# Time mixer of a hybrid decoder block: the triangular inverse in two 32 x 32 blocks a head, with VectorE transposes, and a new order of the units

## The chip, the core and the metric

The kernel runs on one core of a Trainium2 chip. The metric is device time in microseconds of one execution. Engines: TensorE (PE), VectorE (DVE), ScalarE (ACT), GpSimd (POOL) and SyncE (SP), which issues the weight loads. Each works through its own queue in order; semaphores tie them together.

## The reference, cut to what matters

The program is one decoder block on 272 tokens (16 meta tokens and 256) of width 2048: layer norm, a projection, an RWKV-7 time mixer with 32 heads of 64, a causal pooling branch, a gated merge, and an expert channel mixer. The change touches the time mixer alone:

```python
def step(S, inp):
    r_t, w_t, k_t, v_t, kk_t, a_t = inp
    sa = jnp.einsum('bhij,bhj->bhi', S, -kk_t)
    S = (S * w_t[:, :, None, :]
         + sa[..., None] * (kk_t * a_t)[:, :, None, :]
         + v_t[..., None] * k_t[:, :, None, :])
    y_t = jnp.einsum('bhij,bhj->bhi', S, r_t)
    return S, y_t
...
y = rwkv7_scan(r_h, w_h, k_h, v_h, kk, a_h)
ym = jnp.mean(y, axis=-1, keepdims=True)
yv = jnp.mean(jnp.square(y - ym), axis=-1, keepdims=True)
y = ((y - ym) * lax.rsqrt(yv + GN_EPS)).reshape(B, T, RWKV_DIM) * gn_g + gn_b
```

`y_t` is linear in the values `v`, so values with their mean over a head's 64 channels taken out give a `y` with mean zero.

## The kernel before, in words

`rwkv_stage` takes the heads in 16 pairs: two heads fill the 128 partitions, and `by_head` issues one 64 x 64 product for each of them. The 272 tokens are padded to five chunks of 64. Inside a chunk the recurrence is solved in closed form, which needs the inverse of a unit triangular 64 x 64 matrix per chunk and head; from chunk to chunk the state S is carried (units r, u, s).

The inverse is built by doubling. Unit gr makes three grams: B by A (masked into `LT_st`), A by B (the start of the first factor `X_st`) and K by A (masked into `MT_st`). `Y_st`, the second factor, is X's transpose. At level i = 1 to 5 unit Z multiplies `LT_st` by `X_st`, DVE masks the result into `Z_st`, and unit W forms two products, Y by Z, added to `X_st` (not at level 5), and Z by Y, added to `Y_st`. All are 64 columns wide. Levels 4 and 5 leave out the first chunk.

Unit t turns B, K and V (`BKV_by_token`) by a product with the identity; V's product gives tokens by channels. After the chain, unit yc copies y out of PSUM, gm takes its mean by a product with ones (line 704), DVE subtracts it (line 925), ACT squares it (line 794), gv sums the squares (line 708), ge and gy normalise and gate.

Beside this runs the projection: unit f issues one of 16 steps of a tile as three products (line 188, `product`), 48 steps a turn; its weights come in halves that SP loads, ACT rounds (line 152) and DVE takes the remainder of (line 173), unit sp. Units e take a finished tile out of PSUM. Units lw, la, lg, nm, bo are full-width products of the low-rank paths, the norm of k and the bonus; kn, ex, ab are the ACT and DVE work for them.

The order is one table, `ORDER`, written by hand. `schedule` runs over it on each of PE, ACT and DVE, and each engine carries out the units that it knows. `STAGE` says how many turns a pair lags in a unit: f works on pair b while the low-rank units work on b - 1, the inverse on b - 2 and the chain on b - 3:

```python
for b in range(-1, PAIRS + 3):
    for name, i in ORDER:
        p = b - STAGE[name]
        if name in units and 0 <= p < (PAIRS + 4 if name in STREAM else PAIRS):
            units[name](i, p, p % 2)
```

Of the kernel before, what the change touches and what calls it, by code (L numbers as in the profile page):

```python
# [45 lines left out]
C_IOTA = C_LEV + 64 * (LEVELS - 1 + 1)  # L46
NCONST = C_IOTA + 16


# [142 lines left out]
def front_stage(k, w):  # L192

    nc = k.nc
    with ExitStack() as ctx:  # L195
# [265 lines left out]
def rwkv_stage(k, w):  # L461

    nc = k.nc
    with ExitStack() as ctx:
# [1333 lines left out]
```

## Time and profile before

| | |
|---|---|
| median of 3 runs | 2664.82 us (2664.28 to 2665.7) |
| profiled execution | 2663.81 us, span 2661.3 us |
| granted TensorE clock, mean | 0.986 |
| PE busy | 2255.4 us, 85% |
| DVE busy | 1566.4 us, 59% |
| ACT busy | 661.0 us, 25% |
| first and last gram of the time mixer | 102.11 us, 795.44 us |

A profile's rows name a line of the kernel, an engine, an operation and the tiles it writes and reads. PE rows with x20 are 20 instructions: an fp32 product counts as two, and `by_head` issues one for each head. Idle time in brackets is the engine's idle time just before, with what released it. Busy time of PE runs from a product's start to its modelled end, which is later than the start of the next one.

### The profile page before, as it was taken

How to read it: one execution, taken by the hardware profiler on the slowest of the kernel's cores; microseconds unless marked ns; L12 is line 12 of the kernel's file. 1: busy time of each engine (PE TensorE's matmuls, PEld its weight loads, DVE VectorE, ACT ScalarE, POOL GpSimd, SP SyncE). 2: the span in 40 equal slices, each digit the busy share in tenths (PEclk: the TensorE clock that was granted, in tenths of full speed). 3: DMA queues.
4: the chain of work that ended last, by engine and by line, in shares of the span. 5: the costliest groups of instructions: out<-in, count | busy, mean ns of one | idle time of the engine just before them, and what ended most of it. 6: DMA issues, size and time to landing. Idle time of an engine off the chain costs nothing.

```text
span 2661.3 us, 42121 instructions
## 1 busy us (share of the span) xinstructions
PE 2255.4 (85%) x17653; PEld 1593.7 (60%) x17653; DVE 1566.4 (59%) x2588; ACT 661.0 (25%) x1282; POOL 672.1 (25%) x541
## 2 busy tenths in 40 slices
PE   6989888988988999999898879897778778777776
PEld 6888888888887899997764434443223233222222
DVE  7576666667665545545685567666744544444445
ACT  4433333433332344443221111111100100000000
POOL 1000000000000000000154545455554555444442
PEclk9999999999999999999999999999999999999999
DMA  5422223222232676666599999999999999999997
GB/s 183 122 76 69 78 69 88 69 80 69 64 81 73 184 191 186 184 167 239 176 409 409 413 413 418 417 418 420 421 420 420 420 414 415 420 420 420 420 420 307
DMA packets 346507, 710.49 MB, mean 267 GB/s; under 512 B 13832, under 2 KB 270400, under 8 KB 279744
## 3 DMA queue, kind: packets, MB, share of 16 engines
q0 software_dynamic: 74176, 537.01, 48.9%
q1 hardware_dynamic: 271904, 170.59, 22.3%
q8 instruction: 140, 2.29, 0.4%
q14 instruction: 47, 0.39, 0.0%
q10 hardware_dynamic: 240, 0.21, 0.0%
HBM read 705.66 MB, written 2.10 MB: 266 GB/s over the span
## 4 chain that ended last, share of the span: by engine, by line
DMA 32%; PE 13%; DVE 2%; issue 2%; POOL 1%; DVEq 0%; ACT 0%; POOLq 0%; ACTq 0%
DMA down_rows<-in_v_table,experts 30%; PE bank L1534 10%; DMA up_rows<-in_u_table,experts 3%; PE bank L1483 2%; POOL down_rows L1471 1%; POOL up_rows L1465 1%; DVE up_rows L1635 0%; PE bank L1505 0%; ACT diagonal L1587 0%; PE bank L1499 0%; PE bank L1493 0%; DVE one_hot L1171 0%; DVE expert_sides L1177 0%; DVE side_index L1150 0%; DVE side_index L1143 0%
## 5 line engine op out<-in xcount | busy, mean ns | idle before, releaser
L1534 PE MATMUL bank<-down_rows,diagonal 128*128 128x512 f32 x2032 | 947.1, 610 | 246.5 <-DMA down_rows<-in_v_table,experts 210.0
L1635 DVE CUSTOM_DVE_ANT_0 up_rows<-up_rows,h 128x2048 f32<-128x2048 f32 x256 | 585.5, 2291 | 560.6 <-DMA up_rows<-in_u_table,experts 560.6
L1534 PEld LDWEIGHTS bank<-down_rows,diagonal 128*128 128x128 f32 x2032 | 374.1, 192 | 777.9 <-DMA down_rows<-in_v_table,experts 397.0
L1465 POOL DMA_INDIRECT up_rows<-in_u_table,experts x256 | 279.2, 1091 | 1347.4 <-POOLq L1189 1253.0
L1471 POOL DMA_INDIRECT down_rows<-in_v_table,experts x256 | 384.4, 1502 | 570.8 <-PE bank L1534 562.5
L173 DVE TENSOR_TENSOR w_half_rest<-w_half,w_half_high 128x1024 fp32r<-128x1024 f32 x224 | 273.6, 1223 | 260.1 <-ACT w_half_high L152 258.8
L188 PE MATMUL project<-hT_high,w_half_high 128*128 128x272 f32 x896 | 285.7, 319 | 1.4 <-PEq L195 1.4
L152 ACT CAST w_half_high<-w_half 128x1024 fp32r<-128x1024 f32 x224 | 234.4, 1049 | 192.6 <-PE merge_ps L188 163.9
L188 PE MATMUL project<-hT_high,w_half_rest 128*128 128x272 f32 x896 | 259.2, 289 | 0.0
L188 PE MATMUL project<-hT,w_half_high 128*128 128x272 f32 x896 | 258.5, 289 | 0.0
L1605 ACT ACTIVATE dots<-dots 128x4 f32<-128x4 f32 x64 | 13.1, 205 | 743.1 <-DVE dots L1635 743.0
L188 PEld LDWEIGHTS project<-hT_high,w_half_high 128*128 128x128 f32 x896 | 169.3, 189 | 8.8 <-issue 1.6
L188 PEld LDWEIGHTS project<-hT,w_half_high 128*128 128x128 f32 x896 | 169.5, 189 | 4.2
L188 PEld LDWEIGHTS project<-hT_high,w_half_rest 128*128 128x128 f32 x896 | 169.1, 189 | 0.0
L1587 ACT ACTIVATE diagonal<-constants,weights 128x128 f32<-128x128 f32 x256 | 81.9, 393 | 282.3 <-DVE weights L1642 282.3
L188 PE MATMUL merge_ps<-hT_high,w_half_high 128*128 128x256 f32 x512 | 144.5, 282 | 6.1 <-PEq L91 6.1
L188 PE MATMUL merge_ps<-hT,w_half_high 128*128 128x256 f32 x512 | 145.2, 284 | 0.0
L188 PE MATMUL merge_ps<-hT_high,w_half_rest 128*128 128x256 f32 x512 | 145.1, 283 | 0.0
L188 PEld LDWEIGHTS merge_ps<-hT_high,w_half_high 128*128 128x128 f32 x512 | 98.0, 191 | 6.5 <-issue 6.5
L188 PEld LDWEIGHTS merge_ps<-hT_high,w_half_rest 128*128 128x128 f32 x512 | 98.1, 192 | 0.0
L188 PEld LDWEIGHTS merge_ps<-hT,w_half_high 128*128 128x128 f32 x512 | 97.3, 190 | 0.0
L518 PE MATMUL invert<-X_st,LT_st 64*64 64x64 f32 x1472 | 58.6, 221 | 24.4 <-DVE X_st L902 24.2
(314 smaller groups left out, 3157.9 us busy)
## 6 DMA issues: line engine op xcount, KB each, us to landing
w_half<-in_w_in SPq DMA_DIRECT2D x176, 512.0 KB, 4.2
w_half<-in_w_branch_a SPq DMA_DIRECT2D x32, 512.0 KB, 4.1
out_w<-in_w_out SPq DMA_DIRECT2D x16, 1024.0 KB, 5.3
query_w<-in_w_q_peer SPq DMA_DIRECT2D x10, 1024.0 KB, 34.1
w_half<-in_w_branch_b SPq DMA_DIRECT2D x16, 512.0 KB, 4.1
out_w<-in_w_q_peer SPq DMA_DIRECT2D x6, 1024.0 KB, 36.2
up_rows<-in_u_table,experts POOLq DMA_INDIRECT x256, 16.5
down_rows<-in_v_table,experts POOLq DMA_INDIRECT x256, 15.9
```

Of the source, the lines that this page charges most:

```text
L152: self.nc.scalar.copy(self.w_high[g % 3][:].bitcast(F32R), self.w_raw[g % 3][:]).then_inc(self.s_rounded, 1)
L173: return eng.tensor_tensor(low.bitcast(F32R), x, high, ALU.subtract)
L188: mm = nc.tensor.matmul(out, a.bitcast(F32R), b.bitcast(F32R), start=start and n == 0, stop=stop and n == 2)
L518: mm = nc.tensor.matmul(out[h], wts[h], x[h], start=start, stop=stop)
L1465: pool.indirect_dma_start(ur[n % RU][:], None, w["u_table"][0], bass.IndirectOffsetOnAxis(ap=k.idx[:, t, h, j:j + 1], axis=0)).then_inc(s_ ...
L1471: pool.indirect_dma_start(vr[n % RV][:], None, w["v_table"][0], bass.IndirectOffsetOnAxis(ap=k.idx[:, t, h, j:j + 1], axis=0)).then_inc(s_ ...
L1483: mm = nc.tensor.matmul(pq[i][:, 0:SEQ], k.query_part(h, i, kt), k.h1T[:, kt, :], start=(kt == 0), stop=(kt == KT - 1))
L1534: mm = nc.tensor.matmul(acc[t][c][:], dg[n % RD][:], vr[n % RV][:, quarter(c)], start=False, stop=(n == last(t, c)), skip_group_check=True)
L1587: nc.scalar.activation(dg[n % RD][:], ident, ACT.Copy, scale=weights[:, n:n + 1]).then_inc(s_diag, 1)
L1605: nc.scalar.activation(x, x, ACT.Gelu).then_inc(s_gelu, 1)
L1635: v.tensor_tensor_reduce(ur[n % RU][:], ur[n % RU][:], k.h[:, n // (HEADS * TOPK), :], 1.0, 0.0, ALU.mult, ALU.add, dots[:, n:n + 1]).then ...
```

## The change

- The inverse is kept as the two 32 x 32 diagonal blocks of each head, side by side in 32 columns: `X_blocks` and `Y_blocks` are 5 x 32 wide. The A by B gram goes. Level 0 is now a Z product too (against a 32-column identity), and its result, masked, is X; Y is its transpose by `n.transpose`, which turns 32 x 32 blocks on DVE.
- Levels 1 to 4: Z (32 columns), a mask that spreads the result over the two blocks (`Z_st`, 64 columns), one product T (32 columns) added to Y, and X as the transpose of Y. The product Y by Z goes.
- Level 5 uses the off-diagonal block `LT_off`, which ACT cuts from the gram. ACT spreads Y's blocks into the 64-column `Y_st` (unit yf), and T of level 5 is added to its right half.
- The two products on R share one PSUM bank and one mask (`RBKT_st`).
- V is turned by a centring matrix instead of the identity. The mean product, the subtraction and unit gm go; ACT squares y straight from PSUM, before it copies it.
- The units stand in a new order. Unit nm's DVE part is a unit nr of its own.

```diff
+    c[:, C_LEV:C_LEV + CH] = s // HALF == t // HALF
...
+    c[:, C_CEN:C_CEN + CH] = (s == t) - 1.0 / HEAD
...
 ORDER = (
-    ("sp", 1), ("cv", 0), ("gr", 0), ("r", 0), ("t", 0), ("sp", 2), ("f", 6),
-    ("u", 0), ("rb", 0), ("s", 0), ("rk", 0), ("t", 1), ("kn", 0), ("f", 6),
-    ("r", 1), ("Z", 1), ("u", 1), ("lw", 0), ("sp", 3), ("f", 6), ("e", 0),
-    ("s", 1), ("W", 1), ("r", 2), ("Z", 2), ("u", 2), ("la", 0), ("sp", 4), ("f", 6),
-    ("s", 2), ("W", 2), ("r", 3), ("Z", 3), ("u", 3), ("lg", 0), ("sp", 5), ("f", 6),
-    ("ex", 0), ("s", 3), ("W", 3), ("r", 4), ("Z", 4), ("u", 4), ("nm", 0), ("f", 6), ("e", 1),
-    ("s", 4), ("W", 4), ("Z", 5), ("bo", 0), ("yc", 0), ("ahead", 0), ("f", 4),
-    ("ab", 0), ("W", 5), ("gm", 0), ("f", 4), ("gv", 0), ("f", 4), ("ge", 0), ("e", 2), ("gy", 0),
+    ("r", 0), ("gr", 0), ("sp", 1), ("t", 0), ("rb", 0), ("u", 0), ("t", 1), ("Z", 0), ("s", 0), ("sp", 2), ("f", 2),
+    ("lw", 0), ("f", 4),
+    ("Z", 1), ("cv", 0), ("r", 1), ("f", 2),
+    ("la", 0), ("u", 1), ("T", 1), ("f", 7),
+    ("lo", 0), ("kn", 0), ("sp", 3), ("lg", 0), ("s", 1), ("Z", 2), ("r", 2), ("T", 2), ("u", 2), ("f", 3),
+    ("sp", 4), ("nm", 0), ("f", 2),
+    ("s", 2), ("Z", 3), ("r", 3), ("nr", 0), ("T", 3), ("u", 3), ("f", 7),
+    ("s", 3), ("Z", 4), ("ex", 0), ("sp", 5), ("r", 4), ("T", 4), ("u", 4), ("bo", 0), ("f", 1),
+    ("e", 0), ("s", 4), ("Z", 5), ("yc", 0), ("ab", 0), ("f", 2),
+    ("yf", 0), ("gv", 0), ("ge", 0), ("T", 5), ("f", 18),
+    ("e", 1), ("ahead", 0), ("gy", 0), ("e", 2),
 )
...
@@ block.tensor
-                for n, lhs, rh in ((0, bst, ast[par]), (1, ast[par], bst), (2, kst, ast[par])):
+                for n, lhs in ((0, bst), (2, kst)):
                     for c in range(NCH):
-                        mm = by_head(inv[n][:, c * CH:(c + 1) * CH], lhs[:, c, :], rh[:, c, :])
+                        mm = by_head(inv[n][:, c * CH:(c + 1) * CH], lhs[:, c, :], ast[par][:, c, :])
...
-                    mm = by_head(low[:, m * CH:(m + 1) * CH], (bst, kst, vst)[n][:, c, :], turn)
+                    mm = by_head(low[:, m * CH:(m + 1) * CH], (bst, kst, vst)[n][:, c, :], center if n == 2 else turn)
...
                 for c in chunks(i):
-                    mm = by_head(inv[0][:, c * CH:(c + 1) * CH], lt[:, c, :], xs[:, c, :])
+                    mm = by_head(inv[2][:, c * HALF:(c + 1) * HALF], (lto if i == LEVELS - 1 else ltd)[:, c, :], xs[:, c, :] if i else eye)
...
-            def W_(i, p, par):
+            def T_(i, p, par):
                 wait(pe, q["Zst"], p * 5 + i)
                 wait(pe, q["Y"], p * LEVELS + i)
...
-                if i < LEVELS - 1:
-                    for c in chunks(i):
-                        mm = by_head(inv[2][:, c * CH:(c + 1) * CH], ys[par][:, c, :], zs[:, c, :])
-                    mm.then_inc(q["W"], 1)
-                for c in chunks(i):
-                    mm = by_head(inv[1][:, c * CH:(c + 1) * CH], zs[:, c, :], ys[par][:, c, :])
+                for c in chunks(i):
+                    mm = by_head(inv[1][:, c * HALF:(c + 1) * HALF], zs[:, c, :], yb[:, c, :])
...
-            def gm(_, p, par):
-                wait(pe, q["Yc"], p + 1)
-                nc.tensor.matmul(mean_ps, ones, yc[:], start=True, stop=True).then_inc(q["mean"], 1)
...
@@ block.scalar
                 wait(act, q["Yo"], p * 4 + 4)
+                nc.scalar.activation(ysq[:], y_ps, ACT.Square).then_inc(q["sqr"], 1)
                 nc.scalar.copy(yc[:], y_ps).then_inc(q["Yc"], 1)
...
+            def lo(_, p, par):
+                wait(act, q["Z"], p * LEVELS)
+                wait(act, q["maskT"], p + 1)
+                nc.scalar.activation(lto[:], c3(inv[0][:, 0:TP]), ACT.Copy, scale=upper).then_inc(q["off"], 1)
+
+            def yf(_, p, par):
+                wait(act, q["Y"], p * LEVELS + LEVELS - 1)
+                nc.scalar.activation(ys[par][:, :, 0:HALF], yb[:], ACT.Copy, scale=upper)
+                nc.scalar.activation(ys[par][:, :, HALF:CH], yb[:], ACT.Copy, scale=lower).then_inc(q["Yfull"], 1)
...
@@ block.vector
             def Z(i, p, par):
+                if i == 0:
+                    n.tensor_tensor(xs[:], c3(inv[2][:, 0:NCH * HALF], HALF), block_mask(C_M1, NCH), ALU.mult)
+                    d()
+                    n.tensor_tensor(xs[:], xs[:], block_mask(C_M1 + HALF, NCH), ALU.add).then_inc(q["X"], 1)
+                    d()
+                    n.transpose(flat(yb), flat(xs)).then_inc(q["Y"], 1)
+                    return
...
+                n.tensor_tensor(yb[:, c0:], yb[:, c0:], add, ALU.add).then_inc(q["Y"], 1)
+                d()
+                n.transpose(flat(xs, c0), flat(yb, c0)).then_inc(q["X"], 1)
```

Three places of the new order, for a turn in the middle. First PE, from unit s of chunk 1 to unit u of chunk 2, level 2 of the inverse; `chain` is the state's PSUM, `invert` the inverse's. Before:

```order
L518 MATMUL chain<-BKV_by_token 64x64 x2
L518 MATMUL chain<-U,BKV_by_token 64x64 x2
L518 MATMUL invert<-Z_st,Y_st 64x64 x10
L518 MATMUL invert<-Y_st,Z_st 64x64 x10
L518 MATMUL chain<-BKV_by_token,MT_st 64x64 x2
L518 MATMUL chain<-S,A_st 64x64 x2
L518 MATMUL chain<-R_st,S 64x64 x2
L518 MATMUL chain<-RKT_st,BKV_by_token 64x64 x2
L518 MATMUL chain<-RBT_st,U 64x64 x2
L518 MATMUL invert<-X_st,LT_st 64x64 x10
L518 MATMUL chain<-rhs,Y_st 64x64 x2
```

Now:

```order
L535 MATMUL chain<-BKV_by_token 64x64 x2
L535 MATMUL chain<-U,BKV_by_token 64x64 x2
L535 MATMUL invert<-X_blocks,LT_diag 64x32 x10
L535 MATMUL chain<-BKV_by_token,MT_st 64x64 x2
L535 MATMUL chain<-S,A_st 64x64 x2
L535 MATMUL chain<-R_st,S 64x64 x2
L535 MATMUL chain<-RBKT_st,BKV_by_token 64x64 x2
L535 MATMUL chain<-RBKT_st,U 64x64 x2
L535 MATMUL invert<-Y_blocks,Z_st 64x32 x10
L535 MATMUL chain<-rhs,Y_st 64x64 x2
```

T, with 32 columns, stands behind the 20 instructions of unit r, and X's transpose is needed only in the next Z; before, W stood in front of r, and its Z in front of the projection.

Second DVE, the start of the inverse of a pair. Before:

```order
L872 COPY chunk_decay<-decay_prod 128x5
L874 TENSOR_TENSOR LT_st<-invert,constants 128x320
L876 TENSOR_TENSOR X_st<-invert,constants 128x320
L878 TENSOR_TENSOR Y_st<-LT_st,constants 128x320
L879 TENSOR_TENSOR X_st<-X_st,constants 128x320
L881 TENSOR_TENSOR Y_st<-Y_st,constants 128x320
L173 TENSOR_TENSOR w_half_rest<-w_half,w_half_high 128x1024
L885 TENSOR_TENSOR RBT_st<-invert,constants 128x256
```

Now:

```order
L887 COPY chunk_decay<-decay_prod 128x5
L889 TENSOR_TENSOR LT_diag<-invert,constants 128x320
L891 TENSOR_TENSOR MT_st<-invert,constants 128x320
L180 TENSOR_TENSOR w_half_rest<-w_half,w_half_high 128x1024
L895 TENSOR_TENSOR RBKT_st<-invert,constants 128x512
L900 TENSOR_TENSOR X_blocks<-invert,constants 128x160
L902 TENSOR_TENSOR X_blocks<-X_blocks,constants 128x160
L904 STREAM_TRANSPOSE Y_blocks<-X_blocks 128x160
L940 TENSOR_SCALAR S<-chain,chunk_decay 128x64
```

The first STREAM_TRANSPOSE makes Y; the mask of both products on R now stands in front of it.

Third ACT, around the square root of k's norm (`k_rnorm`) and the exponentials (`decay_prod`). Before:

```order
L152 CAST w_half_high<-w_half 128x1024
L758 ACTIVATE decay_prod<-decay_sum 128x320
L759 ACTIVATE decay_prod_inv<-decay_sum 128x320
L760 ACTIVATE decay_prod_prev<-decay_sum_prev 128x320
L781 COPY rhs<-chain 128x64
L785 COPY U<-chain 128x64
L765 ACT_TABLE_LOAD
L765 ACTIVATE k_rnorm<-low_rank 128x320
```

Now:

```order
L159 CAST w_half_high<-w_half 128x1024
L773 ACT_TABLE_LOAD
L773 ACTIVATE k_rnorm<-low_rank 128x320
L789 COPY rhs<-chain 128x64
L793 COPY U<-chain 128x64
L766 ACT_TABLE_LOAD
L766 ACTIVATE decay_prod<-decay_sum 128x320
L767 ACTIVATE decay_prod_inv<-decay_sum 128x320
```

The square root moved ahead of the exponentials, so both load a function table here; another load stands before each of y_rstd (line 814) and decay_sigmoid (line 750).

## Rows read from the trace of the kernel before

**Rows 1.** The page, part 1: busy us, share of the span, instructions.

```profile
PE 2255.4 (85%) x17653; PEld 1593.7 (60%) x17653; DVE 1566.4 (59%) x2588; ACT 661.0 (25%) x1282; POOL 672.1 (25%) x541
```

**Rows 2.** Timeline of PE: start, us; the A,B gram of two turns.

```profile
142.37 0.80 PE L518 MATMUL invert<-A_st,B_st 64*64 64x64 f32 x20
...
795.44 0.80 PE L518 MATMUL invert<-A_st,B_st 64*64 64x64 f32 x20
```

**Rows 3.** Windows: length, busy of PE, PEld, DVE, ACT, POOL, PEclk, DMA share.

```profile
102.11:142.37 40.26, 36.22 (x560) 33.48 (x560) 26.11 (x48) 13.20 (x21) 0.00 (x0) 1.00 0.33 87
142.37:795.44 653.07, 583.52 (x9801) 539.53 (x9801) 443.05 (x863) 251.84 (x515) 0.00 (x0) 1.00 0.28 74
```

**Rows 4.** Waits, 142.37 to 795.44 us: us in total, times, longest.

```profile
PE invert L518 <- DVE X_st L902: 20.1, 14, 1.8
PE chain L708 <- ACT y_square L794: 20.1, 14, 1.5
PE chain L518 <- DVE S L916: 19.6, 28, 1.0
...
PE invert L518 <- DVE LT_st L874: 9.5, 13, 1.0
```

**Rows 5.** Timeline of PE: mean product, a projection group, products of the inverse.

```profile
789.58 0.70 PE L704 MATMUL chain<-y,constants 128*128 128x256 f32 x2
789.93 0.48 PE L188 MATMUL project<-hT_high,w_half_high 128*128 128x272 f32 x1
...
806.71 0.39 PE L188 MATMUL project<-hT_high,w_half_high 128*128 128x272 f32 x1
806.94 0.28 PE L188 MATMUL project<-hT,w_half_high 128*128 128x272 f32 x1
...
808.95 0.29 PE L188 MATMUL project<-hT_high,w_half_rest 128*128 128x272 f32 x1
809.17 0.33 PE L518 MATMUL chain<-BKV_by_token 64*64 64x64 f32 x4
...
809.45 0.75 PE L518 MATMUL invert<-Z_st,Y_st 64*64 64x64 f32 x20
...
810.62 0.28 PE L518 MATMUL chain<-BKV_by_token,MT_st 64*64 64x64 f32 x4
```

**Rows 6.** Timeline: from a product to DVE, from DVE to PE.

```profile
479.50 0.75 PE L518 MATMUL invert<-X_st,LT_st 64*64 64x64 f32 x20
...
480.29 0.49 DVE L895 TENSOR_TENSOR Z_st<-invert,constants 128x320 f32<-128x320 f32 x1 [0.69 <-PE invert L518]
...
505.71 0.41 DVE L902 TENSOR_TENSOR X_st<-X_st,invert 128x256 f32<-128x256 f32 x1
...
506.17 0.68 PE L518 MATMUL invert<-X_st,LT_st 64*64 64x64 f32 x16 [1.79 <-DVE X_st L902]
```

**Rows 7.** Groups by form, 142.37 to 795.44 us: busy, mean ns | idle.

```profile
L173 DVE TENSOR_TENSOR w_half_rest<-w_half,w_half_high 128x1024 fp32r<-128x1024 f32 x84 | 102.6, 1221 | 73.9 <-ACT w_half_high L152 72.5
L852 DVE RECIPROCAL k_rnorm<-k_rnorm 128x320 f32<-128x320 f32 x14 | 30.1, 2153 | 1.4 <-issue 0.4
L895 DVE TENSOR_TENSOR Z_st<-invert,constants 128x320 f32<-128x320 f32 x42 | 20.6, 491 | 20.6 <-PE invert L518 20.6
L742 ACT ACT_TABLE_LOAD x14 | 18.0, 1283 | 6.7 <-PE low_rank L585 6.7
L895 DVE TENSOR_TENSOR Z_st<-invert,constants 128x256 f32<-128x256 f32 x28 | 11.9, 424 | 14.2 <-PE invert L518 14.2
```

**Rows 8.** Timeline of PE in the front stage.

```profile
13.11 1.89 PE L266 MATMUL turn<-constants,x_turned 16*128 16x16 f32 x16 [1.07 <-DVE x_turned L373]
...
33.32 0.43 PE L188 MATMUL lora_project<-hT_high,lora_weights_rest 128*128 128x272 f32 x1
```

**Rows 9.** Timeline of PE in the stage's last turn.

```profile
857.12 0.70 PE L704 MATMUL chain<-y,constants 128*128 128x256 f32 x2 [0.53 <-ACT y L790]
...
860.18 0.70 PE L708 MATMUL chain<-y_square,constants 128*128 128x256 f32 x2 [2.36 <-ACT y_square L794]
```

More of the change, by code:

```diff
@@ L45 @@
 C_LEV = 832
-C_IOTA = C_LEV + 64 * (LEVELS - 1 + 1)
-NCONST = C_IOTA + 16
+C_IOTA = C_LEV + 64 * LEVELS
+C_CEN = C_IOTA + 16
+C_BLK = C_CEN + 64
+NCONST = C_BLK + 2
+HALF = CH // 2
 def constants():
@@ L483, in rwkv_stage @@
         ends = two("chunk_decay", [P, NCH])
-        lt, xs, zs = (sb(n, [P, NCH, CH]) for n in ("LT_st", "X_st", "Z_st"))
+        ltd, lto, zs = (sb(n, [P, NCH, CH]) for n in ("LT_diag", "LT_off", "Z_st"))
+        xs, yb = (sb(n, [P, NCH, HALF]) for n in ("X_blocks", "Y_blocks"))
         mt, ys = two("MT_st", [P, NCH, CH]), two("Y_st", [P, NCH, CH])
-        rbt, rkt, tok = two("RBT_st", [P, 4, CH]), two("RKT_st", [P, 4, CH]), two("BKV_by_token", [P, 3 * NCH - 2, CH])
+        rbk, tok = two("RBKT_st", [P, 8, CH]), two("BKV_by_token", [P, 3 * NCH - 2, CH])
         rhs, u, spc, s = sb("rhs", [P, CH]), sb("U", [P, CH]), sb("S_decayed", [P, CH]), two("S", [P, CH])
@@ L669, in r_ @@
                 if c == 0:
-                    wait(pe, q["Y"], p * LEVELS + LEVELS)
+                    wait(pe, q["mtr"], p + 1)
                     wait(pe, q["tok"], p * 2 + 2)
@@ L892, in Z @@
[L892 to L904 removed]
+                wait(dve, q["gram"], p * 2 + 1)
@@ new lines, in gr, with rb, Z @@
+                n.tensor_tensor(ltd[:], c3(inv[0][:, 0:TP]), mask(C_LEV, NCH), ALU.mult).then_inc(q["maskT"], 1)
+                wait(dve, q["gram"], p * 2 + 2)
+                n.tensor_tensor(mt[par][:], c3(inv[2][:, 0:TP]), mask(C_SU, NCH), ALU.mult).then_inc(q["mtr"], 1)
+            def rb(_, p, par):
+                wait(dve, q["gram2"], p + 1)
+                n.tensor_tensor(rbk[par][:], c3(inv[1][:]), mask(C_IU, 8), ALU.mult).then_inc(q["rbr"], 1)
+            def Z(i, p, par):
+                wait(dve, q["Z"], p * LEVELS + i + 1)
+                if i == 0:
+                    n.tensor_tensor(xs[:], c3(inv[2][:, 0:NCH * HALF], HALF), block_mask(C_M1, NCH), ALU.mult)
[4 more added lines that the diff above has]
+                    return
+                c0 = chunks(i).start
+                z = inv[2][:, c0 * HALF:NCH * HALF].rearrange("p (c b t) -> p c b t", b=1, t=HALF).to_broadcast((P, NCH - c0, 2, HALF))
+                level = k.const[:, C_LEV + CH * i:C_LEV + CH * (i + 1)].rearrange("p (c b t) -> p c b t", c=1, b=2).to_broadcast((P, NCH - c0, 2, HALF))
+                n.tensor_tensor(zs[:, c0:].rearrange("p c (b t) -> p c b t", b=2), z, level, ALU.mult).then_inc(q["Zst"], 1)
@@ new lines, in flat, with T_ @@
+            def flat(x, c0=0):
+                return x[:, c0:, :].rearrange("p c t -> p (c t)")
+            def T_(i, p, par):
+                wait(dve, q["WT"], p * 5 + i)
+                c0 = chunks(i).start
+                add = c3(inv[1][:, c0 * HALF:NCH * HALF], HALF)
+                if i == LEVELS - 1:
+                    wait(dve, q["Yfull"], p + 1)
+                    y = ys[par][:, c0:, HALF:CH]
+                    n.tensor_tensor(y, y, add, ALU.add).then_inc(q["Y"], 1)
+                    return
+                n.tensor_tensor(yb[:, c0:], yb[:, c0:], add, ALU.add).then_inc(q["Y"], 1)
+                d()
+                n.transpose(flat(xs, c0), flat(yb, c0)).then_inc(q["X"], 1)
@@ L920, in s_, with ge @@
                     d()
-            def gm(_, p, par):
+            def ge(_, p, par):
                 n.tensor_copy(gcur[:], k.vec[:, V_GNG:V_GNB + 1, p])
-                wait(dve, q["mean"], p + 1)
-                n.scalar_tensor_tensor(out=yc[:], in0=mean_ps, scalar=-1.0 / HEAD, in1=yc[:], op0=ALU.mult, op1=ALU.add).then_inc(q["center"], 1)
-            def ge(_, p, par):
                 wait(dve, q["vsqrt"], p + 1)
```

100 lines of the change are left out of this document (37 added, 63 removed).

## The prediction

> **What bounds the kernel now.** The page first: TensorE (PE) has matmuls in flight for 85% of the span, VectorE (DVE) is busy for 59% [rows 1]. The change touches only the time mixer, so the second reading cuts out its stretch, 102 to 867 us. From 142.37 to 795.44 us the loop over head pairs turns 14 times, the same work each time: the A,B gram stands at both ends, so one turn is 653.07/14 = **46.65 us** [rows 2]. [...] PE is in order, so a turn is its work plus its waits, here 69.55/14 = 4.97 us. The waits view names four of them: DVE's new state S 1.40 a turn, the inverse's first factor X 1.44, y_square 1.44, the first mask LT_st 0.68 [rows 4]. The bound is PE's issue, with four places where DVE or ACT ends last. The DMA share is 0.28 in this stretch [rows 3]: loads are not the limit.
>
> **Prices.** A 64-column fp32 step of one head is two instructions; 40 of them start between 809.45 and 810.62, 0.0293 us each, so 20 take 0.585 [rows 5]. Inside a projection group 16 steps take 2.01 us (806.94 to 808.95), 0.126 each; the whole group of 18, from 806.71 to 809.17, takes 2.46, so a visit to the projection costs 0.20 us beyond its matmuls [rows 5]. A Z product that starts at 479.50 is issued by 480.08 (20 instructions), DVE starts on it at 480.29, 0.21 us later; DVE's 505.71 + 0.41 lets PE start at 506.17, 0.05 us later [rows 6]. On DVE 320 elements from PSUM take 0.491 us and 256 take 0.424 [rows 7], 1.05 ns an element: I price 160 elements at 0.32 us, 128 at 0.29, 512 at 0.69.
>
> **The sum, for one turn.**
> 1. PE instructions. Gone: one of three grams (20) and the product W (5, 5, 5 and 4 chunks at 4 instructions, 76). New: Z of level 0 (20). Net 76 fewer at 0.0293: **-2.2 us**.
> 2. V is centred by the matrix that turns it, at no price, since that product was issued before too. Gone: the mean product L704, 0.35 us from 789.58 to the next start at 789.93 [rows 5], and DVE's subtraction. The projection is visited 8 times a turn, as before. **-0.35**.
> 3. Z and T now stream 32 columns against 64 x 64 weights: 112 + 92 = 204 instructions. Does the time go by streamed columns or by the weights loaded? Ends: 0.0293 (nothing gained) and half, 0.0146 (-3.0 us a turn). [...]
> 4. The old waits. y_square: the square is now taken straight from PSUM as soon as y is there, and two projection steps stand before the variance product (6 x 0.126 + 0.2 = 1.0 us against 0.21 + 0.42 + 0.05). LT_st: the products on R no longer wait for the first mask but write another bank. X: the new factor is followed by projection before each Z. S: it still stands behind one 1.22 us remainder of a weight half on DVE [rows 7], but the rounding before it now has 15 to 21 matmuls of cover. All four go if this holds: **-4.97**, and about 0.4 of tails that the profile books as busy at a wait.
> 5. New waits. T of level 2, 3 and 4 has no projection before it. From the end of Z's issue the mask is ready after 0.21 + 0.49 + 0.05 = 0.75 us (0.68 at level 4); PE fills that with 20 chain instructions, 0.585. That is 0.17, 0.17 and 0.10, plus a slip of 0.13 at S of chunk 1 behind the remainder, and 0.3 of tails: **+0.9**.
>
> 46.65 - 2.2 - 0.35 - 0.5 - 5.4 + 0.9 = 39.1 us, a saving of 7.55 us, times 14 = **105.7 us**.
>
> The other turns: the one at 102.11 takes 40.26 us with 4.04 of waits [rows 3]; without the chain its three T wait 0.7 each; saving 2.7 + 4.0 - 2.1 = 4.6. For the one at 795.44 I count no old waits, only 3.05 - 0.9 = 2.1. In the last one mean, centring and square stand 3.06 us apart (857.12 to 860.18) with PE idle [rows 9]; about 2.5 go. Total 105.7 + 4.6 + 2.1 + 2.5 = **115 us**. The profiled execution took 2663.81 us, 1.0 less than the median 2664.82, so the forecast is 2664.8 - 115 = **2550 us**.
>
> **What hides the rest.** DVE loses four 320-element operations at the start of the inverse, nine additions, two masks and the centring (7.35 us by rows 7), and gets one 512-element mask, three 160-element operations at level 0, five short additions and four transposes (4.4): 31.6 - 2.9 = 28.7 us busy in 39.1. No row shows a DVE transpose. [...]
> Cover is thin in two places. Before Z of level 4: DVE needs two short operations, some 0.6 together, 2.15 (the reciprocal of k's norm now stands in front of T3's addition), 0.32 + 0.32 and gaps of 0.2 = 3.6 us; PE has T3, u, 21 matmuls and s = 3.8. Before Z5: 1.22 + 0.29 + 0.29 + 0.15 = 1.95 against 2.2. At the end of a turn T5's addition stands behind both the decay products and the whole normalisation. DVE's queue from the last Z mask on: decay products 3.0 us (six operations of 320), normalisation 3.5 (a reciprocal of 256 at the rate of rows 7, 1.7, three operations of 256, a copy, gaps), T5's addition 0.3, ACT's cast and copy in between 0.9, k's shift 0.5, a remainder 1.2, y's remainder 0.4, v's shift 0.5: 10.3 us. PE has the variance product, T5 and 54 matmuls, 8.0. So DVE carries 2.3 us into the next turn; there PE has 7.7 us of grams, turns and projection before Z1, DVE 5.5 of its own, and catches up.
> ACT gets LT_off (some 0.5) and two copies of Y (0.6), and four function table loads a turn instead of two: the square root of k's norm now stands before the exponentials. 2 x 1.283 [rows 7] makes 21.7 us of 39.1, under PE's work as long as ACT comes to each copy of rhs in time.
>
> [...]
>
> **Rivals.**
> A. Streamed columns set the pace (the -3.0 end). For it: a 272-column product takes 0.126 us. [...] It gives 2.5 us more a turn until DVE's chain ends last: 2550 - 35 = 2515.
> B. DVE's chain becomes the bound: a transpose at 0.6 to 0.8 us uses up both thin covers, or table loads make the exponentials and with them the weight remainder late. Each turn then waits 2 us more: 2550 + 32 = 2582. For it: 0.2 us of cover. Against: 10 us of DVE idle in a turn.
> C. The waits move instead of going: X and S waits come back at T and Z, and hold the same 5 us. Only steps 1 to 3 stay, 3.05 x 16 = 49, plus 6 at the two ends: 2610.
> [...]
>
> **The numbers.** Forecast 0.75 (2528 to 2572), A 0.05, B 0.11, C 0.06, D 0.03. The range runs from A's value to beyond B's: 2515 to 2590. A measurement of this kernel tells 0.2% (5 us) from no change; only D ends near or above it: faster 0.96, same 0.01, slower 0.03.
>
> **What would show it.** A turn of 38 to 40 us between two A,B grams; Z and T at 0.027 us an instruction; STREAM_TRANSPOSE at 0.32 us; no PE wait for y_square; short PE waits for Z_st; PE waits in total under 1.5 us a turn. Wrong it would be if X_blocks tops the waits (B), if S and Z_st together hold 4 us a turn (C), or if the granted clock falls below 0.95 in the stage (D).

## The result, and the profile after

The changed kernel takes **2506.28 us** (median of 4 runs, 2505.67 to 2507.12), the kernel before, measured beside it, 2665.26. The ratio is 0.9404, with a 95% interval of 0.9388 to 0.942: 159 us faster. The forecast said 115, and the time lies 9 us below its range.

The page of the changed kernel, part 1, against [rows 1]:

```profile
PE 2193.2 (88%) x16405; PEld 1541.7 (62%) x16405; DVE 1523.8 (61%) x2540; ACT 716.3 (29%) x1357; POOL 668.3 (27%) x541
```

1248 matmuls fewer, 62 us less of PE, and its share rises: the idle time shrank more than the work.

Windows of the changed kernel, cut at the same A,B grams as [rows 3], then up to the merge of the halves behind the mixer, and the expert stage (length, busy of PE, PEld, DVE, ACT, POOL, PEclk, DMA share, GB/s):

```profile
101.58:137.12 35.54, 33.75 (x489) 31.09 (x490) 24.01 (x46) 16.23 (x27) 0.00 (x0) 1.00 0.39 110
137.12:669.13 532.01, 532.01 (x8712) 492.18 (x8712) 407.93 (x824) 304.70 (x585) 0.00 (x0) 1.00 0.33 90
669.13:735.34 66.21, 55.87 (x845) 51.09 (x843) 35.54 (x67) 21.03 (x45) 0.00 (x0) 0.97 0.30 81
1182.00:2504.00 1322.00, 1060.82 (x2636) 480.40 (x2636) 757.06 (x1226) 155.01 (x423) 659.82 (x512) 0.98 1.00 419
```

The expert stage of the kernel before, same view:

```profile
1313.50:2661.00 1347.50, 1067.25 (x2636) 482.03 (x2636) 757.14 (x1226) 154.89 (x423) 663.57 (x512) 0.98 1.00 411
```

Two places changed. In the mixer 14 turns take 532.01 us, **38.00 a turn** where it was 46.65, and PE is booked busy for all of them: no wait of [rows 4] is left. With the first turn (35.54 for 40.26) and the last ones (66.21 for 71.56) that is 131 us. The other 25.5 us lie in the expert stage, which the change does not touch and the forecast called unaffected: 1347.5 us at 411 GB/s became 1322.0 at 419. The stretch between them keeps its length (446.5 us before, 446.7 now), and the two spans, 2661.3 and 2504.0 us, differ by 157.

One turn of PE, worked out from its timeline by adding, for each kind of product, the time from its start to the next start, less the reported idle time (before 375.13 to 421.76, after 403.11 to 441.12):

| us in one turn | before | after |
|---|---|---|
| reported waits | 5.06 | 0 |
| the second product on Y (W), 76 instructions | 2.23 | gone |
| third gram, now Z of level 0, 20 | 0.58 | 0.55 |
| Z of levels 1 to 5, 92 | 2.93 | 2.68 |
| T, 92 | 2.99 | 2.93 |
| mean product | 0.34 | gone |
| projection, 144 products | 20.63 | 19.92 |
| all else, T's short waits in it | 11.87 | 11.93 |
| sum | 46.63 | 38.01 |

Timeline of PE in the changed kernel: Z and T of level 3, then the starts of Z4 and Z5; below them DVE, which makes X for the two (start, us):

```profile
422.90 0.72 PE L535 MATMUL invert<-X_blocks,LT_diag 64*64 64x32 f32 x20
423.45 0.31 PE L535 MATMUL chain<-BKV_by_token,MT_st 64*64 64x64 f32 x4
...
423.95 0.28 PE L535 MATMUL chain<-RBKT_st,U 64*64 64x64 f32 x4
424.21 0.77 PE L535 MATMUL invert<-Y_blocks,Z_st 64*64 64x32 f32 x20
...
428.18 0.61 PE L535 MATMUL invert<-X_blocks,LT_diag 64*64 64x32 f32 x16
428.62 0.31 PE L535 MATMUL chain<-BKV_by_token,MT_st 64*64 64x64 f32 x4
...
431.44 0.61 PE L535 MATMUL invert<-X_blocks,LT_off 64*64 64x32 f32 x16
```

```profile
424.63 2.15 DVE L867 RECIPROCAL k_rnorm<-k_rnorm 128x320 f32<-128x320 f32 x1
426.70 0.26 DVE L924 TENSOR_TENSOR Y_blocks<-Y_blocks,invert 128x160 f32<-128x160 f32 x1
427.05 0.34 DVE L926 STREAM_TRANSPOSE X_blocks<-Y_blocks 128x160 f32<-128x160 f32 x1
...
430.68 0.31 DVE L926 STREAM_TRANSPOSE X_blocks<-Y_blocks 128x128 f32<-128x128 f32 x1
```

Twenty instructions take 0.55 us (422.90 to 423.45), sixteen 0.44 (428.18 to 428.62). A short unit of 4 takes 0.12, so T, starting 0.26 behind the last one, waits about 0.15, which the waits view does not list. X is ready 0.79 us before Z4 starts (427.39, 428.18) and 0.45 before Z5 (430.99, 431.44).

The 0.71 us that the projection loses has to do with its neighbours. Timeline of PE in the changed kernel, the end of two visits to the projection:

```profile
408.49 0.29 PE L195 MATMUL project<-hT_high,w_half_rest 128*128 128x272 f32 x1
408.61 0.62 PE L602 MATMUL low_rank<-lora,w_decay 96*128 96x272 f32 x2
...
410.45 0.29 PE L195 MATMUL project<-hT_high,w_half_rest 128*128 128x272 f32 x1
410.67 0.77 PE L535 MATMUL invert<-X_blocks,LT_diag 64*64 64x32 f32 x20
```

A full-width product starts 0.12 us behind the last projection product, a 64 x 64 one 0.22. In the kernel before, eight of the nine visits of a turn end in front of a 64 x 64 product, and a visit costs 0.19 to 0.41 us beyond its products at 0.126 each, 2.4 in the turn. Now five of ten end in front of a full-width one and cost 0.10, the others 0.18 to 0.32, 1.7 in the turn.

### The profile page after: what moved, and what is told of

The parts are those of the page before. It is cut to its first block, busy times and chain, and to the rows that moved or that the text cites. A ratio compares the mean times of both kernels' runs of the same rounds, so it can differ in the third digit from the quotient of the medians.

```text
span 2504.0 us, 39762 instructions
## 1 busy us (share of the span) xinstructions
PE 2193.2 (88%) x16405; PEld 1541.7 (62%) x16405; DVE 1523.8 (61%) x2540; ACT 716.3 (29%) x1357; POOL 668.3 (27%) x541
## 3 DMA queue, kind: packets, MB, share of 16 engines
q8 instruction: 130, 2.13, 0.3%
## 4 chain that ended last, share of the span: by engine, by line
DMA 32%; PE 15%; DVE 2%; issue 2%; POOL 1%; DVEq 0%; ACT 0%; POOLq 0%; ACTq 0%
DMA down_rows<-in_v_table,experts 29%; PE bank L1552 12%; DMA up_rows<-in_u_table,experts 3%; PE bank L1501 2%; POOL down_rows L1489 1%; POOL up_rows L1483 0%; DVE up_rows L1653 0%; PE bank L1523 0%; PE bank L1511 0%; ACT diagonal L1605 0%; PE bank L1517 0%; DVE one_hot L1189 0%; DVE expert_sides L1195 0%; DVE side_index L1168 0%; DVE side_index L1161 0%
## 5 line engine op out<-in xcount | busy, mean ns | idle before, releaser
L1483 POOL DMA_INDIRECT up_rows<-in_u_table,experts x256 | 289.1, 1129 | 1214.3 <-POOLq L1207 1120.8
L1489 POOL DMA_INDIRECT down_rows<-in_v_table,experts x256 | 370.7, 1448 | 549.7 <-PE bank L1552 541.3
L1501 PE MATMUL bank<-h1T,query_w 128*128 128x256 f32 x256 | 65.1, 388 | 9.4 <-ACT queryT L1575 9.4
```

The source lines that it names most:

```text
L1483: pool.indirect_dma_start(ur[n % RU][:], None, w["u_table"][0], bass.IndirectOffsetOnAxis(ap=k.idx[:, t, h, j:j + 1], axis=0)).then_inc(s_ ...
L1489: pool.indirect_dma_start(vr[n % RV][:], None, w["v_table"][0], bass.IndirectOffsetOnAxis(ap=k.idx[:, t, h, j:j + 1], axis=0)).then_inc(s_ ...
L1501: mm = nc.tensor.matmul(pq[i][:, 0:SEQ], k.query_part(h, i, kt), k.h1T[:, kt, :], start=(kt == 0), stop=(kt == KT - 1))
```

## Experiments

Times are medians; "in the mixer" means between the A,B grams of the run's own trace.

**The expert stage: unused bytes.** The change gives the tile of the constants 1298 columns of 4 bytes instead of 1232, and the program allocates the tiles of gathered rows behind it. No view shows an address; what unused bytes behind the constants do to the time and to the rate of the gather can be measured. One line adds them (8 columns are 32 bytes):

```diff
         k.const = k.sb("constants", [P, NCONST])
+        k.pad = k.sb("pad", [P, 8])
```

Five runs: the kernel before with 32, 64 and 96 unused bytes, the changed kernel with 32, the kernel before with 160. The expectations speak of multiples of 64, 128 and 256 bytes. Where a tile starts was not shown, so only differences count: 96 bytes are 64 more than 32, and 160 are 128 more.

> [...] Theory (the last 26 us of the gain are the transfers' destinations): the time mixer keeps its 46.65 us a turn, the expert stage falls from 1347 to about 1322 us, the total to about 2639 us. Rival (the faster transfers come from something else, the size of the constants in HBM, or the chip's state): 2665 us.

> Control: the kernel before with 64 unused bytes a partition behind the constants. [...] Theory (64-byte boundary of the destination): no change, 2665 us. Rival (any move of the tiles or another neighbour changes the rate): away from 2665 by more than 5 us.

> [...] Theory (a multiple of 64 is enough): as with 32 bytes, about 2639 us. Rival (128 bytes or more are needed): 2665 us.

> [...] Theory: the expert stage goes back to about 1347 us, the time mixer stays at 38.0 us a turn, total about 2506 + 26 = 2532 us. Rival (something else in the change speeds the transfers up): 2506 us.

> [...] Theory: a start at a multiple of 128 bytes is enough, 2640 us as with 32 unused bytes. Rival: it takes 256, and this stands with the 96 unused bytes at 2659 us.

| kernel, unused bytes | us | against the kernel before | GB/s, 1400 to 2400 us |
|---|---|---|---|
| before | 2665 | 1 | 417 |
| before + 32 bytes | 2639.79 | 0.9902 [0.9885, 0.9918] | 425 |
| before + 64 | 2663.49 | 0.9996 [0.9987, 1.0006] | 417 |
| before + 96 | 2659.28 | 0.9979 [0.997, 0.9989] | 419 |
| before + 160 | 2659.56 | 0.9977 [0.9968, 0.9987] | 419 |
| after | 2506.28 | 0.9404 | 426 |
| after + 32 | 2529.22 | 0.9491 [0.9475, 0.9506] | 418 |

The three runs with 32 and 64 unused bytes came out as predicted. The two predicted on the theories of a 64-byte and of a 128-byte multiple missed: 96 and 160 bytes give a fifth of the gain (6 us), only 32 all of it (25 us, and 23 lost in the changed kernel). In these runs the unused bytes stand in front of many tiles, so the last one put them around the rows alone:

```diff
+        sb("pad_before", [P, 8])
         ur = [sb(f"up_rows{i}", [P, D]) for i in range(RU)]
         vr = [sb(f"down_rows{i}", [P, D]) for i in range(RV)]
+        sb("pad_behind", [P, 56])
```

> [...] Theory: the destination address of the gathered rows sets the gather's rate, so this gives the whole loss of the shift behind the constants: 2529 us, rows at 409 to 420 GB/s. Rival: another tile's address did it (the weight halves, the hidden state, the diagonals): 2506 us.

Measured: 2527.53 us (0.9484 [0.9468, 0.95]), 21 us lost. So the place of the rows alone is worth 21 of the 23 us. (Behind the rows the pair adds 256 bytes; 256 bytes more in the constants, the 1296 columns of the centring alone below, left the rate at 420 GB/s, as in the kernel before.) The GB/s line of the page, first the changed kernel, then this one:

```profile
GB/s 193 128 90 85 102 89 85 95 88 93 86 102 194 185 185 185 169 238 140 421 419 423 422 427 423 426 427 427 427 427 427 427 422 426 427 427 428 427 427 307
```

```profile
GB/s 193 125 89 84 101 89 84 101 89 84 94 101 206 186 185 184 142 268 176 416 415 419 415 418 420 411 420 420 420 420 419 421 411 421 419 420 420 420 420 302
```

From the 27th slice on the gather runs mostly at 420 instead of 427 GB/s, and with a DMA share of 1.00 in this stage it sets the pace there.

**The mixer: each part alone.** Three kernels: the kernel before with its own inverse and centring in the new order; the changed kernel in the old order; and the kernel before with only V's centring.

Order alone (a line of the table):

```diff
-    ("s", 2), ("W", 2), ("r", 3), ("Z", 3), ("u", 3), ("lg", 0), ("sp", 5), ("f", 6),
+    ("s", 2), ("Z", 3), ("r", 3), ("nr", 0), ("W", 3), ("u", 3), ("f", 7),
```

Inverse in the old order (against the changed kernel):

```diff
-    ("s", 2), ("Z", 3), ("r", 3), ("nr", 0), ("T", 3), ("u", 3), ("f", 7),
+    ("s", 2), ("T", 2), ("r", 3), ("Z", 3), ("u", 3), ("lg", 0), ("sp", 5), ("f", 6),
```

Centring alone:

```diff
-                    mm = by_head(low[:, m * CH:(m + 1) * CH], (bst, kst, vst)[n][:, c, :], turn)
+                    mm = by_head(low[:, m * CH:(m + 1) * CH], (bst, kst, vst)[n][:, c, :], center if n == 2 else turn)
-                nc.tensor.matmul(mean_ps, ones, yc[:], start=True, stop=True).then_inc(q["mean"], 1)
```

> The kernel before with its own 64-column inverse and its own centring, its units in the new order (Z of level 0 left out, W in the place of T, the two products on R one after the other, the DVE part of the norm of k as a unit of its own; the mean product behind two projection steps, W of level 5 and the variance behind it). Destinations of the transfers as before. Theory (the order removes the waits, whatever the inverse costs): a turn of 46.65 - 5.4 + 0.9 = 42.2 us, total about 2600 us. Rival (the new order holds only with the short inverse, since DVE has 3 us more to do in a turn and two additions behind each W): waits for X_st and S stay near 3 us a turn, total 2640 us or more.

> The changed kernel with its short inverse and its centring in the order of before (T in the place of W, the new units lo, nr and yf put in). [...] Theory (PE work and the waits for y_square and the first mask go with the inverse and the centring, those for X and S with the order): a turn of 46.65 - 3.05 - 1.44 - 0.68 - 0.4 = 41.1 us, total about 2506 + 14 x 3.1 = 2549 us. Rival (the short chain alone removes the waits and the order adds nothing): 2510 us.

> The kernel before with V turned by the centring matrix, without the mean product, the subtraction and their unit, y squared straight from PSUM; inverse and order as before, destinations as before. Theory: 0.35 us of PE and the 1.44 us wait for y_square go from each turn, and 2.5 us in the last one: 14 x 1.9 + 4 = 31 us, total about 2634 us. Rival (the wait moves to the variance product or to S): about 2658 us.

Measured: order alone 2624.53 us (0.9848 [0.9831, 0.9864]), inverse in the old order 2635.4 (0.9885 [0.9869, 0.9902]), centring alone 2633.16 (0.9877 [0.9861, 0.9894]). The centring did what was expected. The order alone gave 40 us, between the two cases: its turns are 43.8 us. The waits for X, S and y_square are gone, as the theory said, but that for the first mask has grown. Its waits of 180.67 to 753 us, and two of its turns in the windows:

```profile
PE invert L521 <- DVE LT_st L877: 26.9, 13, 2.2
```

```profile
353.67:398.37 44.70, 42.51 (x704) 39.32 (x704) 31.71 (x63) 20.80 (x39) 0.00 (x0) 0.96 0.28 78
487.83:531.00 43.17, 40.98 (x705) 37.84 (x704) 31.72 (x63) 20.80 (x39) 0.00 (x0) 1.00 0.30 80
```

In this kernel the product of R and B writes the bank that the mask LT_st still has to read, and in the new order no projection stands between the grams and it: 2.2 us in most turns. In the changed kernel the A by B gram is gone and its bank takes both products on R, so this wait goes only with the new inverse. In eight of the 14 turns the granted clock falls behind this wait, which costs 1.5 us each time.

The inverse in the old order missed by far. Its constants have 1298 columns and its gather runs at 427 GB/s, as in the changed kernel, worth 25 of its 29 us, so in the mixer it gains next to nothing: 46.35 us a turn over 14 turns, and 2 us more than with the centring alone (44.35), which it contains. (The profiled execution took 2640.47 us, 5 more than the median.) Its windows (two neighbouring turns) and its waits of 140 to 798 us:

```profile
426.29:472.79 46.50, 41.85 (x624) 38.60 (x623) 29.57 (x60) 19.03 (x40) 0.00 (x0) 0.93 0.27 75
381.68:426.29 44.61, 40.22 (x624) 37.29 (x623) 29.47 (x60) 19.03 (x40) 0.00 (x0) 0.96 0.28 78
```

```profile
PE invert L532 <- DVE X_blocks L923: 39.4, 53, 2.4
PE chain L532 <- DVE S L935: 22.6, 15, 1.6
```

4.4 us a turn of waits are back, and it is one place above all: Z of level 5 stands directly behind T of level 4 in the old order and waits 2.2 us for addition, drain and transpose; Z of levels 2 to 4, with a unit of chain in between, waits 0.6 together, and S 1.6. Also the granted clock is below 1. Its timeline of PE shows the low stretch:

```profile
443.35 0.33 PE L532 MATMUL chain<-S,A_st 64*64 64x64 f32 x4 [1.55 <-DVE S L935]
...
444.20 0.77 PE L532 MATMUL invert<-X_blocks,LT_diag 64*64 64x32 f32 x20 [0.17 <-DVE X_blocks L923]
...
446.28 0.43 PE L195 MATMUL project<-hT,w_half_high 128*128 128x272 f32 x1
446.51 0.43 PE L195 MATMUL project<-hT_high,w_half_rest 128*128 128x272 f32 x1
...
448.69 0.29 PE L195 MATMUL project<-hT_high,w_half_high 128*128 128x272 f32 x1
448.82 0.29 PE L195 MATMUL project<-hT,w_half_high 128*128 128x272 f32 x1
```

Projection products of 272 columns stand 0.23 us apart instead of 0.13: a granted clock of 0.50 (446 to 448 us) for some 3 us behind the wait of 1.55. The kernel before does the same once, behind its one wait of 1.79 us [rows 6]; that turn in its windows, and its timeline of PE:

```profile
468.39:515.79 47.40, 43.12 (x701) 39.82 (x700) 31.84 (x63) 18.04 (x37) 0.00 (x0) 0.96 0.27 73
```

```profile
506.17 0.68 PE L518 MATMUL invert<-X_st,LT_st 64*64 64x64 f32 x16 [1.79 <-DVE X_st L902]
...
508.13 0.43 PE L188 MATMUL project<-hT_high,w_half_rest 128*128 128x272 f32 x1
508.36 0.43 PE L188 MATMUL project<-hT_high,w_half_high 128*128 128x272 f32 x1
```

Its other 13 turns, with waits up to 1.52 us, read 1.00. Waits or width? This kernel gives the products of Z (levels 1 to 5) and T a second, useless block of 32 columns, which the next product overwrites, all but the last product of each unit; then the same in the changed kernel (the line of T; Z's is changed alike):

```diff
-                    mm = by_head(inv[1][:, c * HALF:(c + 1) * HALF], zs[:, c, :], yb[:, c, :])
+                    w = min(c + 2, NCH)
+                    mm = by_head(inv[1][:, c * HALF:w * HALF], zs[:, c, :], yb[:, c:w, :].rearrange("p c t -> p (c t)"))
```

> The changed inverse in the old order of the units (2635.4 us, clock 0.92 in the turns), with each product of Z (levels 1 to 5) and T streaming 64 columns instead of 32, except the last of a unit: the second half is overwritten by the next product. Same instructions, same waits. Theory: the waits of 2.2 and 1.6 us lower the clock, not the width: the turns stay at 0.92, and the time rises by 144 wider instructions x 0.0017 us x 16 to 2639 us or stays, as the waits shrink by what the products take longer. Rival: the narrow products lower it: the clock returns to 1.00 and some 2 us a turn with it, 2605 us.

> The same widening in the changed kernel. Theory: the loaded columns set the pace, so half the streamed columns are worth 0.0276 against 0.0293 us an instruction, 144 x 0.0017 = 0.25 us a turn: 2506.3 + 4 = 2510 us. Rival: the pace goes by streamed columns once they are the longer part, up to 0.5 us a turn: 2514 us or more.

The rival of the first held for the greater part: more columns streamed, and 2613.97 us (0.9805 [0.9788, 0.9821]), 21 us less where it said 30. Two of its windows, and its waits, 142 to 783 us:

```profile
370.42:414.66 44.24, 38.93 (x623) 35.87 (x623) 29.49 (x60) 19.08 (x40) 0.00 (x0) 1.00 0.28 78
640.95:687.08 46.13, 41.72 (x623) 38.56 (x623) 29.60 (x60) 19.07 (x40) 0.00 (x0) 0.93 0.27 75
```

```profile
PE invert L532 <- DVE X_blocks L925: 39.1, 56, 2.4
PE chain L532 <- DVE S L937: 34.4, 26, 1.6
```

The same waits and more, and a clock of 1.00 in nine turns of 14; in the last five it reads 0.93 to 0.96, as in the kernel with narrow products, where no turn of the 14 reads 1.00. So the width counts (0.92 became 0.98 over the 14 turns), but wide products do not keep the clock up behind such waits. In the changed kernel the widening costs nothing: 2504.44 us (0.9395 [0.9379, 0.941]), 37.99 us a turn. Timeline of PE of that kernel, Z of level 3:

```profile
421.77 0.72 PE L535 MATMUL invert<-X_blocks,LT_diag 64*64 64x64 f32 x20
422.33 0.31 PE L535 MATMUL chain<-BKV_by_token,MT_st 64*64 64x64 f32 x4
```

0.56 us with 64 columns, 0.55 with 32, and in a whole turn Z and T take the same 5.6 us in both kernels. My theory there was wrong too, in the cheap direction: half the columns saves nothing inside a unit.

Could the projection's place repair the old order? The changed inverse in the old order, with half of a projection group moved between each T and the next Z:

```diff
-    ("s", 1), ("T", 1), ("r", 2), ("Z", 2), ("u", 2), ("la", 0), ("sp", 4), ("f", 6),
+    ("s", 1), ("T", 1), ("r", 2), ("f", 3), ("Z", 2), ("u", 2), ("la", 0), ("sp", 4), ("f", 3),
```

> The changed inverse and centring in the old order (2635.4 us), with the projection group of levels 2 to 5 cut in two: half of its steps now stand between T with the addition behind it and the next Z. Four more visits to the projection, 0.8 us a turn. Theory: X's waits in front of Z (2.7 us a turn) go, and with the idle times the stretches at half clock (about 2 us a turn) too: net 3 to 4 us a turn, 2580 us. Rival: the clock stays low (narrow products, not idle times, lower it) and S waits 1.5 us as before, only X's waits go: 2 us a turn, 2605 us. Second rival: nothing moves but the waits, 2635 us.

It did none of what was expected: 2711.72 us (1.0167 [1.0127, 1.0206]; its four times lie between 2696 and 2718), slower than the kernel before, and 76 us slower than without the split. One turn in its windows, and its waits from 147 to 868 us:

```profile
400.50:455.19 54.69, 48.49 (x623) 44.02 (x623) 29.41 (x60) 19.01 (x40) 0.00 (x0) 0.81 0.23 63
```

```profile
PE chain L532 <- DVE S L935: 59.1, 38, 2.5
PE invert L532 <- DVE X_blocks L923: 33.3, 14, 2.6
```

Its timeline of DVE, in front of such an S (PE starts on it at 426.34 after 2.13 us of waiting):

```profile
424.69 1.22 DVE L180 TENSOR_TENSOR w_half_rest<-w_half,w_half_high 128x1024 fp32r<-128x1024 f32 x1
426.00 0.28 DVE L935 SCALAR_TENSOR_TENSOR S<-chain,chunk_decay,S_decayed 128x64 f32<-128x64 f32 x1
```

The X waits of levels 2 to 4 (0.6 a turn before the split) are gone, that of Z5 stayed at 2.4 a turn, and S waits 59.1 us in all, 4.2 a turn: the projection decides not only what PE does meanwhile but when the next part of a weight half's rounding enters DVE's queue, and the 1.2 us remainder now stands in front of the new state. With that the clock falls to 0.81 in this turn, and to 0.88 over the 14.

**The mean restored in the new order** completes the parts: the changed kernel with the identity for V, mean product and subtraction.

```diff
-    ("yf", 0), ("gv", 0), ("ge", 0), ("T", 5), ("f", 18),
+    ("gm", 0), ("ab", 0), ("yf", 0), ("T", 5), ("f", 6), ("gv", 0), ("ge", 0), ("f", 12),
```

> The changed kernel without its centring: V is turned by the plain identity again, the mean product and VectorE's subtraction are back, with the square behind them; order and inverse stay the changed kernel's, except that the mean product stands two projection steps behind y and the variance product eight. Theory: the centring's 31 us in the old order were mostly waits (y_square), so in the new order, where projection stands between, it is worth the mean product and one more visit to the projection, 0.55 us a pair: 2506.3 + 16 x 0.55 = 2515 us. Rival: it is worth the same in either order, 2537 us.

Measured 2541.56 (0.9538 [0.9522, 0.9554]), 35 us lost: the rival. The mean product takes 0.52 us of the 2.2 a turn and its visit to the projection 0.2; two new waits hold 1.1, of PE for ACT's copy of B, K and V by token (12.8 us in 12 turns) and for DVE's mask MT_st (3.1 in 13). The variance product gives 0.28 back, and the rest is short tails, 0.4 of them in the product of V and in u, and two turns with a clock of 0.96. Turn lengths (mean of the 14 turns of each trace), all parts together:

| us a turn | old order | new order |
|---|---|---|
| old inverse, mean | 46.65 | 43.8 |
| old inverse, V centred | 44.35 | not tried |
| new inverse, mean | not tried | 40.2 |
| new inverse, V centred | 46.35 (45.0 with wide products) | 38.0 |

**How much cover VectorE and ScalarE have.**

```diff
+                for _ in range(3):
+                    n.transpose(flat(xs, c0), flat(yb, c0))
+                    d()
                 n.transpose(flat(xs, c0), flat(yb, c0)).then_inc(q["X"], 1)
```

> The changed kernel with each transpose of levels 1 to 4 done twice over, 0.35 + 0.09 us more on DVE at each level, 1.7 us a turn. Theory (my thin covers of 0.2 us in front of Z of level 4 and 5): two waits of 0.2 to 0.3 us a turn come up, total about 2513 us. Rival 1 (more cover than I worked out): 2506 us. Rival 2 (DVE's chain is the bound already): 15 x 1.7 = 26 us more, 2532 us.

> The changed kernel with each transpose of levels 1 to 4 done four times: 1.1 us more in VectorE's chain at each level, 4.5 us a turn. Twice cost nothing. Theory: the cover that was worked out (0.2 us before Z of level 4 and 5, more before the others) is too small by something under 1 us, so now Z of level 4 and 5 wait 0.5 to 1 us each: 1 to 2 us a turn, 2525 us. Rival: the cover is over 1.1 us everywhere, 2506 us.

> The changed kernel with ScalarE's exponentials in front of the norm's square root again: two function table loads a turn instead of four, 2.6 us less of ScalarE a turn. Theory: TensorE's record has no reported wait in the turns, ScalarE is off the path, so nothing: 2506 us within 5. Rival: ScalarE's copies of rhs are late behind the table loads and sit in TensorE's unreported gaps (some 0.1 us at T): up to 0.3 us a turn, 2501 us.

Twice: 2506.21 us, no change. Four times: 2543.15 (0.9537 [0.9521, 0.9553]), 37 us more where 19 were expected: 2.15 us in each of 14 turns, and 6.7 in the first one, which had not been counted. Waits of that kernel, 143 to 705 us:

```profile
PE invert L535 <- DVE X_blocks L929: 13.9, 28, 0.7
PE chain L535 <- DVE S L941: 7.4, 14, 0.6
```

Two Z a turn wait, up to 0.7 us, for a chain made 1.1 us longer, which agrees with the 0.79 and 0.45 us of slack read above; S waits another 0.5 a turn, which nobody expected. Fewer table loads: 2506.01 us, no change; ScalarE is off the path.

**The granted clock in all of these kernels**, over the 14 turns of each trace, from the windows of single turns:

| kernel | columns of Z and T (W) | waits a turn, us | longest | turns below 1.00 | mean clock |
|---|---|---|---|---|---|
| before | 64 | 5.0 | 1.8 | 1 | 1.00 |
| centring alone | 64 | 3.5 | 1.4 | 0 | 1.00 |
| order alone | 64 | 1.9 | 2.2 | 8 | 0.98 |
| inverse, old order | 32 | 4.5 | 2.4 | 14 | 0.92 |
| the same, wide | 64 | 5.3 | 2.5 | 5 | 0.98 |
| the same, projection split | 32 | 6.6 | 2.6 | 14 | 0.88 |
| mean restored | 32 | 1.1 | 1.1 | 2 | 0.99 |
| transposes four times | 32 | 1.5 | 0.7 | 0 | 1.00 |
| changed, and changed wide | 32, 64 | 0 | 0 | 0 | 1.00 |

In the order alone, turns with the same products and the same wait of 2.17 us read 1.00 four times and 0.96 eight times. So neither the longest wait nor the width decides it by itself; what does is not settled.

## Why the prediction was right or wrong

1. **"The change touches only the time mixer" failed**, and with it went 25 us. The constants grew by 66 columns (NCONST in the full diff), and the gather of 537 MB of rows ran at 427 GB/s instead of 420, as it does in the kernel before with 32 unused bytes; the changed kernel with 32 unused bytes falls back to 420. That the larger constants moved the rows' destination is the author's reading: no view of the trace shows an address. With the slow gather the time is 2529 (measured, + 32 bytes), inside the range. That the change ended on the fast side is luck.
2. **Step 1** (76 fewer instructions, -2.2): measured -2.26, W's 2.23 and 0.03 for the gram. Right.
3. **Step 2** (mean product, -0.35): -0.34. The projection is not visited "8 times a turn, as before": there are nine visits before and ten now. The sum booked y_square's wait elsewhere; the centring with its waits is worth 2.3 us a turn in the old order and 2.2 in the new.
4. **Step 3** (Z and T, -0.5): no run shows this term or the 0.027 us an instruction behind it. The runs showed -0.31 in the table, and not as a price of an instruction. Twenty instructions take 0.55 us instead of 0.58 for a gram of 64 columns, and sixteen take 0.44 instead of 0.47: 0.03 less for each unit, however long it is. The starts of the single instructions agree: inside a unit two of them stand 0.058 us apart at 32 and at 64 columns, and only the pair at one end is 0.027 shorter. Ten units of 0.03 are the 0.31. In the widened kernel the last product of each unit stayed at 32 columns, and it keeps the 0.03: 0.56 us for twenty with 64 columns, 0.55 with 32. An instruction costs 29 ns inside a unit, 27.7 as the mean of twenty.
5. **Step 4** (all four old waits go, -4.97, tails -0.4): the waits are -5.06 by the view, as forecast. The tails were undersized: the projection's 144 products, whose instructions and number did not change, take 0.71 less, although there is one visit more. The prediction booked 0.20 us for any visit; the traces show 0.10 to 0.41, with the low price where full-width products follow, so new neighbours change it.
6. **Step 5** (new waits, +0.9) **was, with the tails of step 4, the term that failed in the mixer**. T of levels 2, 3 and 4 waits 0.15, 0.15 and 0.06 us, together 0.36 where 0.44 was forecast: this part is right. What is left of steps 4 and 5 beyond the named waits (tails -0.4 and +0.3, a slip of 0.13 at S) was forecast at nothing, and measured at -1.0: the 0.71 of the projection, and 0.3 in "all else", where three full-width products that now stand in front of 64 x 64 ones take 0.55 more and the other ends 0.85 less. Steps 1 to 5 together: 39.1 forecast, 38.0 measured, 14 x 1.1 = 15 us. Of the 44 us by which the forecast missed, 25 are the gather and 15 this term; the rest lies in the two ends and between medians and profiled executions.
7. **Cover.** Both thin places had more room than worked out: 0.79 us instead of 0.2 before Z4, 0.45 instead of 0.2 before Z5. The transposes cost 346 ns for 160 columns and 313 for 128 where 0.32 was taken. VectorE came to 29.1 us a turn (28.7 forecast, from 31.6 before), ScalarE to 21.8 (21.7 forecast, from 18.0) [rows 3].
8. **Rivals.** A (columns) is refuted by the wide kernel. B needs over 0.45 us more of VectorE at Z5; doubling the transposes did not reach it. C did not happen in the new order and is what the inverse does in the old one. D, given 0.03 (a lower clock of PE), did not happen either: PEclk 1.00. The 1.00 over 653 us in [rows 3] is no proof against it, being a rounded mean: right behind the 1.79 us wait [rows 6] the kernel before does fall to a granted clock of 0.50, for some 3 us. In the changed kernel the waits are gone, and with them the falls. The split kernel shows the price of a low clock, 0.88 over its turns and a time above the kernel before; how much of that its narrow products cause, and how much its waits of 6.6 us a turn, it does not tell.
9. **Ends**: the first turn -4.7 (-4.6 forecast), the last ones -5.35 (-4.6).

## What to carry to other kernels

An edit that changes a tile's size can change the rate of a transfer that it does not touch: compare the GB/s of the bulk gathers before and after, and try 32 unused bytes and a few multiples of them in front of their tiles, which was worth 25 us one way and 23 the other here. A shorter product in a dependent chain is worth its time only if the work around it is placed anew: the same inverse cost 2 us a turn in the old order and gained 3.6 in the new one (1.9 of it the wait for LT_st), so forecast an edit and its schedule together, and look at what the moved filler triggers on the other engines' queues. When products get narrower, remove the waits between them at the same time: the narrow ones with 4.5 us of waits a turn had a clock below 1.00 in every turn. And a mean clock of 1.00 over a long stretch can hide a fall: look at single turns.

## What the runs showed of the hardware

The rate of the gather of 8 KB rows into SBUF changed with unused bytes allocated ahead of them: in the kernel before 420 GB/s with none and with 64, 427 with 32 (the steady slices of the page); with 96 and 160 the whole kernel was 6 us faster than with none, and 20 slower than with 32. In the changed kernel it was 427 with none and 420 with 32; with 32 directly in front of the rows, 21 us were lost. That the start address decides is the author's reading; no run shows one. Products of 64 x 64 fp32 weights cost 29 ns an instruction inside a unit at 32 and at 64 streamed columns alike. A 64 x 64 product started 0.22 us behind a projection product, a full-width one 0.12. TensorE's granted clock stayed at 1.00 without waits, with products of either width; it fell to 0.50 for some 3 us or more behind single waits of 1.1 to 2.6 us, in all 14 turns with narrow products and 4.5 us of waits a turn, in 5 of 14 with the same waits and wide products, in 8 of 14 with wide products and one wait of 2.2 us, in 1 of 14 in the kernel before, behind its one wait of 1.8, and in none with wide products and waits up to 1.4 us. Which of these it answers to is not settled by these runs.
